# Attention in place and one unit deeper, copies all on ScalarE, query blocks 0, 3, 2, 1, and filler matmuls

## The reference

```python
s_c = einsum('bqhd,bcd->bhqc', qn, k_cmp) * scale
p_c = masked_softmax(s_c, cmp_end[None, :] <= tq[:, None])
...
s_s = einsum('bqhd,bqkd->bhqk', qr, kg) * scale
...
s_w = einsum('bqhd,bkd->bhqk', qr, kwb) * scale
...
s = einsum('bthd,bmhd->bhtm', q, mem_k) * (MEM_HEAD_DIM ** -0.5)
```

```python
score = einsum('bqh,bhqs->bqs', wb, relu(einsum('bqhd,bsd->bhqs', qib, k_idx)))
score = where(causal[None], score, -inf)
_, sel = top_k(score, topk)
...
p = softmax(logits, axis=-1)
o = einsum('bqgrk,bqkgd->bqgrd', p, v_sel)
```

## Time and profile before

| what | us |
|---|---|
| median of 3 runs | 2140.89 |
| lowest, highest | 2128.39, 2145.9 |
| the profiled execution, its time | 2129.25 |
| the profiled execution, its span | 2127.3 |
| TensorE busy in it | 1922.6 |
| VectorE busy | 973.7 |
| ScalarE busy | 824.1 |
| GpSimd busy | 259.9 |

### The profile page before, as it was taken

The page is one execution under the profiler, slowest core; times in us unless marked ns, Lnnn a source line. Parts: engine busy times, 40 slices in busy tenths (PEclk is TensorE's granted clock), DMA queues, the critical chain, the costliest instruction groups (busy, mean ns, idle before and its releaser), DMA issues. The chain is left out here.

```text
span 2127.3 us, 31283 instructions
## 1 busy us (share of the span) xinstructions
PE 1922.6 (90%) x12332; PEld 1519.9 (71%) x12332; DVE 973.7 (46%) x1686; ACT 824.1 (39%) x1304; POOL 259.9 (12%) x209
## 2 busy tenths in 40 slices
PE   5999389879978889998799999989999889999997
PEld 4887189745547646667688888868888768888885
DVE  2343835473354588834333333345555443333233
ACT  4223244433223443323444442246565244344322
POOL 3000223110003150000200000022222030000000
PEclk9999579865569995558799999989999899999998
DMA  4321100000002110002122333322222113322331
GB/s 169 98 90 45 38 5 3 29 17 1 1 22 84 50 31 1 1 1 60 60 91 96 99 94 100 94 72 88 73 71 60 41 60 99 99 94 94 99 99 50
DMA packets 37762, 131.66 MB, mean 62 GB/s; under 512 B 4817, under 2 KB 5137, under 8 KB 37393
## 3 DMA queue, kind: packets, MB, share of 16 engines
q1 hardware_dynamic: 36784, 127.91, 19.0%
q10 hardware_dynamic: 864, 2.17, 0.3%
HBM read 127.17 MB, written 2.10 MB: 61 GB/s over the span
## 5 line engine op out<-in xcount | busy, mean ns | idle before, releaser
L138 DVE TENSOR_TENSOR big_parts<-ring,big_parts 128x1024 fp32r<-128x1024 f32 x164 | 205.1, 1252 | 526.8 <-ACT big_parts L133 526.8
L156 PE MATMUL bank<-h_parts,big_parts 128*128 128x512 f32 x960 | 381.9, 398 | 26.0 <-POOL y_parts L1402 17.6
L157 PE MATMUL bank<-y_parts,big_parts 128*128 128x512 f32 x960 | 377.8, 394 | 0.0
L158 PE MATMUL bank<-h_parts,big_parts 128*128 128x512 f32 x960 | 377.5, 393 | 0.0
L133 ACT ACTIVATE big_parts<-ring 128x1024 fp32r<-128x1024 f32 x164 | 173.7, 1061 | 289.2 <-PE bank L158 289.0
L156 PEld LDWEIGHTS bank<-h_parts,big_parts 128*128 128x128 f32 x960 | 182.9, 191 | 67.3 <-issue 28.3
L158 PEld LDWEIGHTS bank<-h_parts,big_parts 128*128 128x128 f32 x960 | 182.7, 190 | 38.5
L157 PEld LDWEIGHTS bank<-y_parts,big_parts 128*128 128x128 f32 x960 | 183.1, 191 | 37.3
L157 PE MATMUL bank<-y_parts,work_parts 128*128 128x512 f32 x456 | 181.4, 398 | 0.0
L138 DVE TENSOR_TENSOR work_parts<-ring,work_parts 128x1024 fp32r<-128x1024 f32 x65 | 79.3, 1223 | 168.0 <-ACT work_parts L133 168.0
L995 ACT ACTIVATE work<-work 128x256 f32<-128x256 f32 (+4 forms) x128 | 67.1, 525 | 209.7 <-DVE work L1013 209.6
(11 more groups left out here) (399 smaller groups left out, 3121.3 us busy)
## 6 DMA issues: line engine op xcount, KB each, us to landing
ring<-in_wstream SPq DMA_DIRECT2D x229, 512.0 KB, 3.5
x<-in_xt SPq DMA_DIRECT2D x4, 512.0 KB, 7.9
out_t<-x SPq DMA_DIRECT2D x8, 256.0 KB, 2.0
work<-in_memt ACTq DMA_DIRECT2D x1, 1024.0 KB, 15.4
work<-in_cw SPq DMA_DIRECT2D x1, 1024.0 KB, 5.1
cst<-in_cst ACTq DMA_DIRECT2D x1, 704.0 KB, 7.9
cos<-in_reset SPq DMA_DIRECT2D x2, 256.0 KB, 2.6
big<-work SPq DMA_DIRECT2D x4, 128.0 KB, 4.0
```

What stands on the lines that cost most here:

```text
L138: dve.tensor_tensor(self.parts[:, self.place_of(n), 1, :, :], self.ring[:, n % RING, :, :], self.parts[:, self.place_of(n), 0, :, :].bitca ...
L156: pe.matmul(out, w[0], x[0], start=start, stop=False, skip_group_check=True)
L157: pe.matmul(out, w[0], x[1], start=False, stop=False, skip_group_check=True)
L158: return pe.matmul(out, w[1], x[0], start=False, stop=stop, skip_group_check=True)
```

## The change

Five things are changed in `Attend` and its two users.

- In place: the maximum writes into the buffer in which the exponential then works. There are five buffers of weights and four of turned weights in place of three, three and three. The maximum of unit n no longer waits for an exponential, but for the transposes of unit n-5.
- One unit deeper: the transposes of a unit are three turns behind its scores, the sums four (before two and three).
- All copies of turned weights are ScalarE's, behind the exponential of the same turn.
- Fillers: `warm` issues n matmuls of 128x128 by 512 columns of constants into the bank that the next transposes overwrite. The sparse stage has five ahead of the transposes of unit 0; the top-k stage has one ahead of the transposes of each of the units 4 to 15.
- The top-k stage takes its query blocks in the order 0, 3, 2, 1, and so do the indexer and the picks.

```diff
+def warm(c, pe, bank, n):
+
+    for _ in range(n):
+        pe.matmul(bank[:, :], con(c, "ident"), c.cst[:, 0:4, :], start=True, stop=True)
...
     SCORES, TURNED, OUT = (0, 1, 2), (3, 4, 5), (6, 7)
-    ROLL = 3
+    WEIGHTS, TURNS = 5, 4
+    TURN, SUM = 3, 4
...
-        self.s = [wk(c, at + i * T, T) for i in range(3)]
-        self.e = [wk(c, at + (3 + i) * T, T) for i in range(3)]
-        self.t = [wk(c, at + (6 + i) * T, T) for i in range(3)]
+        self.e = [wk(c, at + i * T, T) for i in range(self.WEIGHTS)]
+        self.t = [wk(c, at + (self.WEIGHTS + i) * T, T) for i in range(self.TURNS)]
...
+    def tensor_turn(self, pe, n):
...
+        if 0 <= n - self.TURN < len(units):
+            i = n - self.TURN
+            b = c.bank[self.TURNED[i % 3]]
+            if i >= 3:
+                pe.wait_ge(self.copied, i - 2)
+            warm(c, pe, b, self.fill.get(i, 0))
+            self.wait_weights(pe, i)
+            for j, w in units[i].parts:
+                mm = pe.transpose(b[0:w, j:j + P], self.weights(i)[:, j:j + w], con(c, "ident"))
+            mm.then_inc(self.turned, 1)
+        if 0 <= n - self.SUM < len(units):
+            i = n - self.SUM
+            u, g, at = units[i], i // self.group, i % self.group * HD
+            pe.wait_ge(self.copied, i + 1)
...
+    def scalar_turn(self, act, n):
+        units = self.units
+        if n < len(units):
+            act.wait_ge(self.maxed, n + 1)
+            e = self.weights(n)
+            act.activation(e, e, ACT.Exp, bias=self.low[:, n:n + 1], scale=-1.0, accum_out=self.den[:, n:n + 1])\
+               .then_inc(self.exped, 1)
+        if 0 <= n - self.TURN < len(units):
+            i = n - self.TURN
+            act.wait_ge(self.turned, i + 1)
+            if i >= self.TURNS:
+                act.wait_ge(self.summed, i - self.TURNS + 1)
...
+            act.activation(self.t[i % self.TURNS][0:w, 0:cols], self.c.bank[self.TURNED[i % 3]][0:w, 0:cols], ACT.Copy)\
+               .then_inc(self.copied, 1)
...
+            if n >= self.WEIGHTS:
+                dve.wait_ge(self.turned, n - self.WEIGHTS + 1)
...
-    at = Attend(c, "na", units, 8576, 4, finishes)
+    at = Attend(c, "na", units, 8576, 4, finishes, {0: 5})
...
-    items = [(q, h) for q in range(1, QT) for h in range(IH)]
+    late = (3, 2, 1)
+    items = [(q, h) for q in late for h in range(IH)]
...
-    for q in range(QT):
+    for q in (0, *late):
         keys = (q + 1) * P
...
-    at = Attend(c, "da", units, 8 * T, 8, finishes)
+    at = Attend(c, "da", units, 8 * T, 8, finishes, {n: 1 for n in range(4, 16)})
...
-                q = n // (TOPK // 8) + 1
-                if q < QT:
+                if n < len(late) * TOPK // 8:
+                    q = late[n // (TOPK // 8)]
```

More of the change, by code:

```diff
@@ L987, in scalar @@
-    def scalar(self, act):
-        units = self.units
-        for n in range(len(units) + 2):
-            if n < len(units):
-                u = units[n]
-                act.wait_ge(self.maxed, n + 1)
-                if n >= 3:
-                    act.wait_ge(self.turned, n - 2)
-                act.activation(self.e[n % 3][:, 0:u.keys], self.s[n % 3][:, 0:u.keys], ACT.Exp, bias=self.low[:, n:n + 1],
-                               scale=-1.0, accum_out=self.den[:, n:n + 1]).then_inc(self.exped, 1)
-            if 0 <= n - 2 < len(units) and self.by_act(n - 2):
-                self.turn_copy(act, n - 2)
@@ new lines, in tensor_turn @@
+        if n < len(units):
+            u = units[n]
+            if n >= 3:
+                pe.wait_ge(self.maxed, n - 2)
+            scores = c.bank[self.SCORES[n % 3]][:, 0:u.keys]
+            if isinstance(u.q, tuple):
+                mm = product(pe, scores, u.q, u.k, True, True)
+            else:
+                mm = pe.matmul(scores, u.q, u.k, start=True, stop=True)
+            mm.then_inc(self.scored, 1)
+        if 0 <= n - self.TURN < len(units):
[8 more added lines that the diff above has]
+            mm.then_inc(self.turned, 1)
@@ new lines, in tensor_turn @@
+        if 0 <= n - self.SUM < len(units):
+            i = n - self.SUM
+            u, g, at = units[i], i // self.group, i % self.group * HD
+            pe.wait_ge(self.copied, i + 1)
+            if g >= 2 and at == 0:
+                pe.wait_ge(self.finished, g - 1)
+            out = c.bank[self.OUT[g % 2]]
+            for x, (j, w) in enumerate(u.parts):
+                for half in (0, HD):
+                    mm = pe.matmul(out[half:half + HD, at:at + HD], self.t[i % self.TURNS][0:w, j + half:j + half + HD],
+                                   u.vals[x], start=x == 0, stop=x == len(u.parts) - 1, skip_group_check=True)
+            mm.then_inc(self.summed, 1)
@@ L1034, with turns @@
+    def turns(self):
+        return range(len(self.units) + self.SUM)
 NC = (T - 32) // 16 + 1
@@ L1214, in _ @@
         def _(pe):
-            at.tensor(pe)
+            for n in at.turns():
+                at.tensor_turn(pe, n)
             for q in range(QT):
@@ L1224, in _ @@
         def _(act):
-            at.scalar(act)
+            for n in at.turns():
+                at.scalar_turn(act, n)
             act.wait_ge(o_sem, 2)
@@ L1230, in _ @@
         def _(dve):
-            at.vector(dve)
+            for n in at.turns():
+                at.vector_turn(dve, n)
             dve.wait_ge(at.finished, len(finishes))
@@ L1971, in pick @@
                         ch.link(dve.tensor_scalar(v["mask"][:, q, 0:w], s, -2e38, -1e30, ALU.is_gt, ALU.mult))
-            at.vector(dve, pick)
+            for n in at.turns():
+                pick(n)
+                at.vector_turn(dve, n)
             for q in range(QT):
```

120 lines of the change are left out of this document (33 added, 87 removed).

## The result

The changed kernel takes 2163.77 us (median of 4 runs, 2159.91 to 2168.15), the kernel before 2138.68 us in the same job (4 runs). The ratio is 1.0131, 95% interval 1.0103 to 1.0159: slower by 1.3%. Its profiled execution took 2164.94 us with a span of 2162.8.

A forecast was written before the change was run, and what follows sets the result against it. Both attention stages were taken as bound by TensorE's own stream at half clock. Terms 4 + 21.6 + 1.2 + 2 - 1 = +28 us gave 2157 over the profiled execution, 2169 over the median; forecast 2160, range 2070 to 2178.

The forecast's parts named there:

- the likeliest case: Both attention stages stay at half clock, as summed: 2160 us, chance 0.54.
- Step 1: Sparse stage: five fillers ahead of the first transpose take 6.9 us, three cold and two warm, a delay of about 6.4.
- Step 2: Sparse stage after the fillers: warm clock gives 2.6 us back, then half clock; stage sum +4 us.
- step 5: Both stages: in place, one unit deeper, copies to ScalarE; worth 0 at half clock (-1 to +2), lets turns halve at full.
- Step 3: Top-k stage: one filler ahead of each transpose of units 4 to 15; stays cold, 12 x 1.8 = +21.6 us.
- step 4: Block order 0, 3, 2, 1: +1.2 us in top-k turns 0 to 6, output transposes +2, indexer -1.
- The first rival: Top-k stage: single fillers raise the clock near 815 us, stage -55 instead of +24, total 2077; chance 0.17.

The follow-up runs named there:

- the run with units 16 to 19: Changed kernel with one filler ahead of each of top-k units 16 to 19 and none anywhere else; 2092.26 us, ratio 0.9808.

## Why the prediction came out

The forecast was 2160 and the measurement 2163.8; the likeliest case, half clock in both stages, is what happened. That the two times are within 4 us is in part luck: the forecast stands on the kernel before at 2129 to 2141, and in this job that kernel took 2138.7. The difference is the better test, +28 against +25.1.

**Step 1, the row of five.** Predicted a delay of 6.4 us up to the first transpose; measured 5.6 (1.96 us after the stage's first score before, 7.52 now). The five fillers take 6.1 us against 6.9: the clock rose at 471.5, after two cold ones, so that it was two at 1.71 and three at 0.86 and not the other way round. The two durations, estimated from the earlier trace rows, fit.

**Step 2, what it gives back.** Predicted 2.6 us, and half clock again before the 256-key units. Measured: clock at 1.00 from 471.5 for 6.8 us, down at 478.3, given back 3.8 us by unit 8, +1.8 for the whole stage against +4. Against the same stage without fillers it is +2.7 (148.01 there); the rest, -0.9, is step 5's. The reason given, that 31-key units are too thin to hold the clock, fits the sorted stage: same units, same row of five, but behind the 31-key units instead of ahead of them, and the clock holds for 68.3 us. It isn't separated from block 0's one-part units of 128 keys: in the changed kernel their scores already stand in these turns, and in the sorted one they too are ahead of the row.

**Step 3, twelve single fillers.** Predicted 12 x 1.8 = +21.6 us with turns of 3.4 to 3.5 and no rise. Measured 3.46 against 1.65, 12 x 1.81 = 21.8; the fillers alone are worth 20.2, since without them these turns would wait for VectorE's picks (step 4). Right in size and in direction, and the runs sharpen the reason. "Here every filler stands between scores of 64 rows, a transpose and sums of 64 columns" was the argument against a rise; the same filler one unit later, with four transposes behind it instead of one, raised it in two traces, and in a third the one behind it did. The other half of that argument, that the 512-key turns stayed at 0.50 although full, says nothing against a filler in such a turn, as the run with units 16 to 19 shows. The first rival (a rise near 815) priced the warm stage at 2077, 52 us under the kernel before. The kernels in which it warms in every run have medians of 2089 to 2095 (the deeper ones), by the ratios 41 to 46 us under theirs, and no filler in the sparse stage. With the 2.7 us of that row the price was some 9 to 14 us too good: it takes warm turns for half, but a four-part turn goes from 3.67 to 2.09 and a one-part turn of 128 keys from 1.64 to 1.00, both with TensorE busy almost throughout; at full clock TensorE's small instructions take more than half their time (a score part of 512 columns 0.39 against 0.62).

The Trainium skill's rule cited there ("TensorE: Matmul & The Clock Gate", Part 1, that activity releases the throttle) fits these traces only if activity is more than being busy: the change's top-k stage is busy 187.96 of 194 us at 0.50. The other half of that paragraph, that the trace agrees if transposes don't count, is more than the rows bear: of a four-part turn of 3.67 us at half clock the transposes take 1.05, the rest is other matmuls. No run here separates them, since a four-part turn has more of both.

**Step 4, the order of the blocks.** Predicted +1.2 for the turns beside the 512-score picks, by a pace of 1.83 us. Measured pace 1.73, but +2.1 up to unit 7's scores (9.51 us from the first pick before, 11.62 now). The missing part is a wait that no step named. VectorE and ScalarE at the head of the changed stage:

```profile
814.20 0.69 DVE L1960 MAX8 work<-work 128x8 f32<-128x512 f32 x1
...
816.05 0.40 ACT L977 ACTIVATE work<-work 128x128 f32<-128x128 f32 x1 [1.24 <-DVE work L999]
816.35 0.19 ACT L977 ACTIVATION_READ_ACCUMULATOR work<-work 128x1 f32 x1
816.45 0.26 ACT L986 ACTIVATE work<-bank 128x128 f32<-128x128 f32 x1
```

The first copy (L986) is ready long before but stands in ScalarE's queue behind unit 3's exponential, which waits for that unit's pick and maximum on VectorE; the first sum waits 2.84 us for it (816.75, shown above). Step 5 had said that the copy queues behind the next exponential and that this is hidden; in steady state it is, at the head of the stage it isn't. The tail came out as predicted: +1.9 against +2, since the output transposes behind the stage run at half clock:

```profile
1001.41 6.61 PE L1909 MATMUL bank<-cst,h 128*128 128x128 f32 x32 [0.86 <-DVE h L1878]
```

They took 3.71 us before. The indexer came to +1.1 where -1 (-3 to +2) was taken. In all the top-k stage is +25.3 where steps 3 and 4 had taken 22.8 for it.

**Step 5, in place, deeper, copies on ScalarE.** Predicted 0 at half clock. The sparse stage shows it by itself, since its order isn't changed: without fillers it takes 147.1 to 148.4 us in the six kernels with the deeper class and 148.8 to 149.0 in the three with the old one, so some -1. In the top-k stage step and order come together: without fillers it takes 171.35 us against 166.20, +5.2. Of these, 3.0 are longer waits of TensorE (7.6 us against 4.6), and the wait for the first copy alone is 2.8. With the indexer (+1.1) and the tail (+1.8) that makes up the 5.8 us by which this kernel is slower; how much of the 5.2 is step 5's stays open. "At full clock it is what lets the turns halve" was wrong: the shallow class also runs four-part turns in 2.09 and 2.23 us, alternately, once the clock holds.

The sum: +28 predicted, +28.4 measured between the profiled executions without the unrelated 7.1 at the start of the sparse stage. The terms are less good than the sum: the top-k stage was put 2.5 us too low and the indexer 2.1, the sparse stage 2.2 too high, and between and behind the stages the changed kernel was 1.7 us shorter, which no step had. That these cancel to within 1 us is luck.

## What to carry to other kernels

Filler matmuls are worth nothing by themselves: they pay where they lift the clock just ahead of a long dense stretch. Here twelve that end with the last one-part turn cost 20 us of the top-k stage, and four that begin with the first four-part turn gain some 50 against the kernel without fillers. So put the thin work first, the fillers at the border, and the dense work after it, in one piece. Time such an edit in several runs: a kernel near the border shows one of two times, and a single run or profile tells only one of them. A row of five with single fillers behind it, at 0.9 us each at full clock, held in all of 13 runs of three kernels here; a row of five alone at unit 13 or 14 held in 6 of 14.

## What the runs showed of the hardware that was not expected

- One filler in a dense turn raised the clock (838.33; the sum at 840.94 already takes 0.34 us) after 35 us at half clock, in another kernel the second one did (817.06); twelve in thin turns never did.
- A raised clock stayed up although TensorE was not always busy: 82.96 of 86 us, in dense turns without a filler, and 105.05 of 110 in the shallow class. The same stage stays low at 165.23 of 171 us without fillers, and the shallow class at 99.00 of 99 once the clock has fallen. Once up it stays up on work that would not have raised it.
- Whether it holds can differ from run to run of one kernel: 2085 to 2093 and 2147; 2052 to 2055 and 2103 to 2110; 2094 and 2138 to 2144; 2055 to 2068 and 2095.
- The clock fell 2.2 us behind the end of a stall of 1.58 us in one kernel and stayed up behind one of 0.96 us at the same sum in another. That the length of the stall is what decided is a guess: the two kernels also differ in their fillers.
